# A joint norm factor, context squares moved, and filler matmuls in a two-block transformer kernel

## The reference

```python
def rmsnorm(t, g):
    y = t32 * lax.rsqrt(jnp.mean(t32 * t32, axis=-1, keepdims=True) + EPS)
    return (y * g).astype(t.dtype)
# first block, per layer
px = (rmsnorm(x, norm1_g[l]) * (1.0 + sc1) + sh1) @ w_in[l] + b_in[l]
pc = (rmsnorm(xc, norm1_g[l]) * (1.0 + scc1) + shc1) @ w_in[l] + b_in[l]
# ... mLSTM in both directions, spatial gating, convolution -> y_x, y_c
x = x + g1 * (y_x @ w_out[l])
x = x + g2 * swiglu(rmsnorm(x, norm2_g[l]) * (1.0 + sc2) + sh2, w_gu[l], w_down[l])
# the context gets the same, but not in the block's last layer
return rmsnorm(x, final_g)            # end of the first block
# second block: starts with that x and a new context ctx_2; per layer
hx = _rms(x, norm_mix_w[l]) * (1.0 + scx1) + shx1
hc = _rms(ctx, norm_mix_w[l]) * (1.0 + scc1) + shc1
# ... attention -> x = x + gx1 * ax; x = x + gx2 * _swiglu(...)
```

## Time and profile before

| | us |
|---|---|
| median of 3 runs | 2315.93 (2315.74 to 2325.12) |
| the profiled execution | 2320.48 |
| its span, first to last instruction | 2319.0 |
| mean granted TensorE clock | 0.965 of 2.4 GHz |

### The profile page before, as it was taken

One profiled execution on the slowest core, in us unless ns is written; L12 is line 12 of the kernel. 1 busy time (PEld: TensorE's weight loads), 2 busy tenths in 40 slices (PEclk: granted clock), 3 DMA queues, 4 the chain that ended last, 5 costly groups with the idle time before them and its releaser, 6 DMA issues.

```text
span 2319.0 us, 28203 instructions
## 1 busy us (share of the span) xinstructions
PE 2172.9 (94%) x11748; PEld 1663.5 (72%) x11748; DVE 1100.9 (47%) x1927; ACT 855.5 (37%) x1320; POOL 63.8 (3%) x66
## 2 busy tenths in 40 slices
PE   5999789999999898699979999999999989998999
PEld 2766566777776776699966447677777767747999
DVE  4293854323233666655563433432323355556555
ACT  2434233222222553544444243322222344355443
POOL 1000010000001000100010001000000100000000
PEclk7999789999999999899989999999999999999999
DMA  9553023554446524446535002355344322202564
GB/s 355 172 218 109 1 73 127 172 159 160 163 129 218 161 91 138 136 151 203 161 108 179 35 1 73 127 172 157 125 164 130 107 73 91 73 1 92 177 206 126
DMA packets 263216, 308.08 MB, mean 133 GB/s; under 512 B 5425, under 2 KB 250417, under 8 KB 250801
## 3 DMA queue, kind: packets, MB, share of 16 engines
q1 hardware_dynamic: 258384, 301.62, 39.9%
q10 hardware_dynamic: 4704, 4.65, 0.6%
HBM read 305.21 MB, written 1.05 MB: 132 GB/s over the span
## 4 chain that ended last, share of the span: by engine, by line
PE 86%; DVE 7%; ACT 3%; issue 2%; DMA 1%; POOL 1%; ACTq 0%; POOLq 0%; DVEq 0%
PE bank L458 85%; DVE scratch L1093 1%; POOL yT L435 1%; DVE yT L1093 1%; DVE big L1093 1%; PE bank L467 1%; DMA xT<-p_ctx 1%; DVE weights_low L1101 1%; ACT weights_high L1777 1%; DVE input_low L1093 0%; DVE big L1612 0%; ACT rstd L1803 0%; DVE big L1508 0%; DMA parameter_columns<-p_columns 0%; ACT rstd L1805 0%
## 5 line engine op out<-in xcount | busy, mean ns | idle before, releaser
L458 PE MATMUL bank<-input_high,weights_high 128*128 128x512 f32 (+1 forms) x2336 | 826.3, 354 | 37.1 <-DVE input_low L1093 28.1
L458 PE MATMUL bank<-input_low,weights_high 128*128 128x512 f32 (+1 forms) x2336 | 811.6, 347 | 0.0
L458 PE MATMUL bank<-input_high,weights_low 128*128 128x512 f32 (+1 forms) x2336 | 810.4, 347 | 0.0
L1101 DVE TENSOR_TENSOR weights_low<-weight_slots,weights_high 128x1024 fp32r<-128x1024 f32 (+2 forms) x420 | 461.1, 1137 | 413.0 <-ACT weights_high L1777 412.1
L458 PEld LDWEIGHTS bank<-input_high,weights_high 128*128 128x128 f32 x2336 | 444.8, 190 | 153.1 <-issue 71.6
L458 PEld LDWEIGHTS bank<-input_high,weights_low 128*128 128x128 f32 x2336 | 444.1, 190 | 61.2
L458 PEld LDWEIGHTS bank<-input_low,weights_high 128*128 128x128 f32 x2336 | 444.8, 190 | 58.0 <-issue 1.0
L1777 ACT ACTIVATE weights_high<-weight_slots 128x1024 fp32r<-128x1024 f32 (+2 forms) x420 | 386.3, 967 | 177.6 <-PE bank L458 164.6
L458 PE MATMUL bank<-hidden_high,weights_high 128*128 128x256 f32 (+1 forms) x704 | 239.3, 340 | 0.5 <-DVE weights_low L1101 0.5
L458 PE MATMUL bank<-hidden_low,weights_high 128*128 128x256 f32 (+1 forms) x704 | 237.4, 337 | 0.0
L458 PE MATMUL bank<-hidden_high,weights_low 128*128 128x256 f32 (+1 forms) x704 | 237.2, 337 | 0.0
(11 more groups left out here) (230 smaller groups left out, 1570.3 us busy)
## 6 DMA issues: line engine op xcount, KB each, us to landing
modulation_slots<-w_mod SPq DMA_DIRECT2D x48, 1024.0 KB, 5.0
modulation_slots<-mod_w SPq DMA_DIRECT2D x48, 1024.0 KB, 5.0
weight_slots<-w_gu SPq DMA_DIRECT2D x44, 1024.0 KB, 5.1
weight_slots<-ffn_w_in SPq DMA_DIRECT2D x44, 1024.0 KB, 5.1
weight_slots<-w_in SPq DMA_DIRECT2D x24, 1024.0 KB, 5.5
weight_slots<-w_down SPq DMA_DIRECT2D x16, 768.0 KB, 4.9
weight_slots<-ffn_w_out SPq DMA_DIRECT2D x16, 768.0 KB, 5.0
weight_slots<-od_w_in SPq DMA_DIRECT2D x12, 1024.0 KB, 5.2
```

The lines of the kernel that those rows point to most:

```text
L458: return pe.matmul(o, w, r, start=start, stop=stop, skip_group_check=shared)
L1101: tt(m.w_low[:, g % 2, c], m.ring[:, g % SLOTS, c], m.w_high[:, g % 2, c].bitcast(F32), ALU.subtract).then_inc(m.low_made.sem, 1)
```

## The change

1. `add_squares` and `join_squares` take the semaphores of the squares as a parameter and can carry two kinds of sums (`sq_sum` has two rows).
2. A new function `keep_busy(b, n)` on TensorE issues n float32 matmuls of the 1/1024 matrix with the identity (128 by 128) into a bank that nobody reads: 8 at the start, 12 after the sums in each turn of 512 tokens and after feed forward 1, 9 after mixers 1 and 3.
3. The context's squares are made by ScalarE in hidden tiles 4 to 11 of layer 1 (one per tile); their sum stands before the second part of the down projection, their root at its head.
4. At the end of layer 1 two kinds of squares are made per block, of x and of x times the final gain. VectorE forms EPS*(s1+EPS)+s2 from the two means; one Ln and Exp of that is the joint factor of both norms, and layer 2's x gains are multiplied with the final gain. x itself is scaled by its final norm later, in projection tiles 4 to 11 of layer 2, with a root taken after layer 2's `normed`.
5. At the start the two inputs have a semaphore each; squares, joins and sums are made per half, the sums behind modulation steps 4 and 6. The first half of the second weight item goes from before `normed` into it.

```diff
-        self.sq_sum = self.yT[:, 6, :]
+        self.sq_sum = self.yT[:, 6:8, :]
...
-    join_squares("first", slice(0, TOK))
+    for half, t in enumerate((X, C)):
+        join_squares(("first", half), t, m.first_squared)
...
-        join_squares(("out", L), n)
+        join_squares(("out", L), n, m.squared)
         if L == 1:
-            join_squares("context", C)
+            join_squares("context", C, m.squared)
         if L < 3:
-            join_squares(("ffn", L), n)
-        if L == 1:
-            join_squares("final", X)
+            join_squares(("ffn", L), n, m.squared, 2 if L == 1 else 1)
...
+    def add_squares(place, t, squared=m.squared, banks=(7,)):
+        n = len(banks)
         pe.wait_ge(*m.square_joined.end(place))
+        for q, b in enumerate(banks):
+            mm(bank[b][:, t], m.mean_d[:, :], m.sq_sum[:, q, t], True, False)
+        for q, b in enumerate(banks):
+            i = n * (KD - 1) + q
+            pe.wait_ge(*squared.at(place, i))
+            mm(bank[b][:, t], m.mean_d[:, :], yT[:, 2 + i % 4, t], False, True).then_inc(m.square_added.sem, 1)
+
+    def keep_busy(b, n):
+
+        for _ in range(n):
+            mm(bank[b][:, 0:P], m.mean_d[:, :], ident[:, :], True, True)
...
         add_squares(("out", L), slice(0, n))
+        keep_busy(6, 12 if n == TOK else 9)
...
         hidden(L, range(6, 11))
+        if L == 1:
+            add_squares("context", C, banks=(6,))
         down(L, 1)
-        if L < 3:
+        if L == 1:
+            add_squares(("ffn", L), X, banks=(7, 5))
+            keep_busy(4, 12)
+        elif L < 3:
             add_squares(("ffn", L), slice(0, n))
+            keep_busy(5, 12)
...
     for k in range(KD):
         mod_step(k)
-        if k == 5:
-            add_squares("first", slice(0, TOK))
+        if k in (4, 6):
+            add_squares(("first", k // 2 - 2), (X, C)[k // 2 - 2], m.first_squared)
     pe.wait_ge(*m.columns_in.end(0))
     mod_turn(0)
+    keep_busy(6, 8)
...
             if part and f == KD - 2 and L < 3:
                 gains(L + 1, 0)
+                if L == 1:
+                    dve.wait_ge(*m.gains.at(2, 0))
+                    tt(m.coef[:, 0, 0, :], m.coef[:, 0, 0, :], column(G_TAB, FINAL_G, KD), ALU.mult).then_inc(m.gains.sem, 1)
...
+    def final_scaled(k):
+
+        if k == 0:
+            dve.wait_ge(*m.root.at("final", 1))
+        muladd(xT[:, k, X], xT[:, k, X], column(G_TAB, FINAL_G + k), m.final_r, ALU.mult, ALU.mult).then_inc(m.final_scaled.sem, 1)
...
+            if 4 <= e < 12:
+                final_scaled(e - 4)
...
     def even_mixer(L):
-        normed(0, L, TOK, "final", m.proj[L][1], "context")
+        dve.wait_ge(*m.square_added.at(("ffn", 1), 0))
+        ts(rs[:, X], bank[7][:, X], EPS, EPS, ALU.add, ALU.mult).then_inc(m.final_var.sem, 1)
+        dve.wait_ge(*m.square_added.at(("ffn", 1), 1))
+        dve.wait_ge(*m.final_var.at(0, 0))
+        tt(rs[:, X], rs[:, X], bank[5][:, X], ALU.add).then_inc(m.final_var.sem, 1)
+        normed(0, L, TOK, ("ffn", 1), m.proj[L][1], "context")
...
-    low_weights(1, range(1))
...
-    dve.wait_ge(*m.root.at(("ffn", 1), 1))
-    for k in range(KD):
-        muladd(xT[:, k, X], xT[:, k, X], column(G_TAB, FINAL_G + k), rs[:, X], ALU.mult, ALU.mult).then_inc(m.final_scaled.sem, 1)
...
+    def two_squares(f):
+
+        for q in range(2):
+            i = 2 * f + q
+            if i >= 4:
+                act.wait_ge(*m.square_joined.at(("ffn", 1), 2 * max(0, f - 3) + q))
+            F(yT[:, 2 + i % 4, X], xT[:, f, X], ACT.Square, scale=column(G_TAB, FINAL_G + f) if q else 1.0).then_inc(m.squared.sem, 1)
+
+    def final_roots():
+
+        act.wait_ge(*m.final_var.end(0))
+        F(rs[:, X], rs[:, X], ACT.Ln).then_inc(m.root.sem, 1)
+        act.wait_ge(*m.root.at(("ffn", 1), 0))
+        F(rs[:, X], rs[:, X], ACT.Exp, scale=-0.5).then_inc(m.root.sem, 1)
...
+                if L == 1 and 4 <= f < 4 + KD:
+                    if f == 4:
+                        act.wait_ge(*m.context_in.end(0))
+                    square("context", f - 4, C)
...
+        if part and L == 1:
+            rstd("context", C, 6)
...
+        if L == 1:
+            down(L, 1, two_squares)
+            final_roots()
+            return
...
     def even_mixer(L):
         normed(0, L, TOK, m.proj[L][1])
+        final_root()
...
-        if L == 1:
-            act.wait_ge(*m.context_in.end(0))
-            for k in range(KD):
-                square("context", k, C)
         feed_forward(L)
-    for k in range(KD):
-        act.wait_ge(*m.final_scaled.at(0, k))
-        square("final", k, X)
-    rstd("final", X, 5)
```

More of the change, by code:

```diff
@@ L313, in signals @@
         self.biased, self.gains = S("modulation_thirds_biased", *((l, 3) for l in layers)), S(
[L314 to L326, removed]
+            "norm_gains_made", (0, 4), (1, 4), (2, 5), (3, 4))
+        halves = [("first", half) for half in range(2)]
+        order = [("out", 0), ("ffn", 0), ("out", 1), "context", ("ffn", 1), ("out", 2), ("ffn", 2), ("out", 3)]
+        kinds = {p: 2 if p == ("ffn", 1) else 1 for p in halves + order}
+        self.first_squared = S("first_squares_made", *((p, KD) for p in halves))
+        self.squared = S("squares_made", *((p, KD * kinds[p]) for p in order))
+        self.square_joined, self.square_added = S("squares_joined", *((p, (KD - 2) * n) for p, n in kinds.items())), S(
+            "squares_added", *kinds.items())
+        self.final_var = S("final_variances", (0, 2))
+        self.root = S("rstd_steps", *((p, 2) for p in [
+            "first", ("out", 0), ("ffn", 0), ("out", 1), "context", ("ffn", 1), "final", ("out", 2), ("ffn", 2), ("out", 3)]))
         normed = [x for L in layers for x in (
@@ L1129, in gains, with normed @@
                    ALU.mult).then_inc(m.gains.sem, 1)
-    def normed(which, L, n, place, second, also=None):
+    def normed(which, L, n, place, second, also=None, halves=range(1, 2)):
         part, per = (("mix", "ffn")[which], L), n // SEQ
@@ L1153, in normed @@
             if i == 2 * per - 1:
-                low_weights(second, range(1, 2))
+                low_weights(second, halves)
         for i in range((KD - 1) * per, KD * per):
@@ L1734, in vector_program @@
     dve.memset(m.evac_scale[:, K_T:K_T + 4], HD ** -0.5).then_inc(m.consts.sem, 1)
-    dve.wait_ge(*m.input_in.end(0))
-    for k in range(KD):
-        if k >= 4:
-            dve.wait_ge(*m.square_joined.at("first", max(0, k - 5)))
-        tt(yT[:, 2 + k % 4, :], xT[:, k, :], xT[:, k, :], ALU.mult).then_inc(m.first_squared.sem, 1)
+    for half, t in enumerate((X, C)):
+        dve.wait_ge(m.inputs_in[half], 16)
+        for k in range(KD):
+            if k >= 4:
+                dve.wait_ge(*m.square_joined.at(("first", half), max(0, k - 5)))
+            tt(yT[:, 2 + k % 4, t], xT[:, k, t], xT[:, k, t], ALU.mult).then_inc(m.first_squared.sem, 1)
     low_weights(0)
@@ L1809, in coming_weights, with normed @@
             next_weights(m.proj[L][(e + 1) // 2])
-    def normed(which, L, n, second):
+    def normed(which, L, n, second, halves=range(1, 2)):
         part, per = (("mix", "ffn")[which], L), n // SEQ
@@ L1820, in normed @@
             if i == per - 1:
-                high_weights(second, range(1, 2))
+                high_weights(second, halves)
     def gate_activations(L):
@@ L2184, in scalar_program @@
     ln_exp_tables()
+    act.wait_ge(*m.square_added.end(("first", 0)))
+    act.wait_ge(*m.square_added.end(("first", 1)))
     rstd("first", slice(0, TOK))
```

56 lines of the change are left out of this document (22 added, 34 removed).

## The result

The changed kernel takes 2297.9 us (median of 4 runs, 2296.7 to 2298.3); the kernel before, beside it, 2319.7 (4 runs, 2315.7 to 2325.1). The ratio is 0.9899, 95% interval 0.9881 to 0.9918: 1.0% faster. The forecast was 2291.0 (2282 to 2302).

What follows compares the result with a forecast made beforehand. TensorE, busy 94% of the 2319.0 us span, and its clock were taken to bound the kernel. Terms summing to 24.9 us took 2320.5 to 2295.6, less 4.55 for the median: 2291.0 us, range 2282 to 2302.

Steps and rivals of the forecast that it cites:

- Rival (a): In the turns: the filler doesn't hold the clock, so only 13.5 to 14 us stay, giving 2302 us; chance 0.10.
- The terms for mixer 0, mixer 2 and feed forwards 0 and 2: Restarts behind these turns: held clock gains 2.1, 2.5, 0 (VectorE bounds it) and 1.7 us.
- mixer 3's: Restart behind mixer 3: held clock gains 0.8 us (0 to 1.6), with one 0.6 us stall for a VectorE weight half.
- rival (b): In the gaps: filler at 0.73 us each outlasts the waits and blocks, costing 33 us, giving 2324 us; chance 0.03.
- a sign of being wrong: At the restarts: the prediction is wrong if the first product follows a filler without idle.
- the term of -0.9: Layer 1's second down projection: the moved context sum and ScalarE's root cost 0.9 us (0.4 to 1.8).
- rival (c): Layer 1's hidden tiles: Square forces ScalarE table loads between Silus, hidden but for about 2 us, 2293 us; chance 0.02.
- The turn was sized at 8.8: Turn from layer 1's feed forward to layer 2: the joint factor brings the first product 8.8 us earlier, at 1174.9.
- its clock at 1.9: Behind the joint turn: half of 3.84 us of low clock goes, gaining 1.9 us.
- The step that failed: Layer 1's second down projection: 8 more squares and 6 additions fit 3.5 us periods of which ScalarE uses half, unpriced.
- a sign that came out 0.6 us late: Layer 2's start: first product about 7 us after the last down product instead of 15.7.
- Rival (d): In the mLSTM gaps: shifted work meets half clock elsewhere, either sign, 10 us at the bad end, 2301 us; chance 0.07.

Runs made afterwards that it cites:

- the two-norm version: Changed kernel with the joint factor undone: final norm applied and its own squares taken after layer 1's feed forward, 12 fillers behind each sum; 2306.4 us.
- the two experiments on it: Changed kernel with ScalarE's squares put behind the next high weights, 2298.7 us; changed kernel with GpSimd's second-kind additions cut to one column, 2295.7 us.
- the version with small additions: Changed kernel with GpSimd's additions of the second kind of square in layer 1's feed forward cut to one column, sums left incomplete; 2295.7 us.

## Why the prediction came out as it did

- **Clock and filler.** Right: 0.237 us each for 0.25 estimated, 1.00 behind all seven turns with VectorE's wait left over, and 8.5 us lost in the restarts, 10.3 in all stretches, where the filler is taken away. Rival (a), that it doesn't hold the clock, is refuted by the pair of clock rows. The terms for mixer 0, mixer 2 and feed forwards 0 and 2 are within 0.35 us; mixer 3's, 0.2 for 0.8, allowed VectorE one stall of 0.6 us, where the trace has 0.73 and slower steps behind it (0.92 and 0.81 us for the 0.7 assumed). The filler's half-clock price stood in rival (b), "the filler blocks"; not foreseen is where it is met: 0.47 us each at the start and 0.39 in the two-norm version. There (b) is real, on a scale of 1 us and not of 33. That the first product at the start then follows a filler without idle is a sign of being wrong that did occur, in that one place.
- **Context squares.** Right to 0.1 us in the turn and to 0.15 in the term of -0.9. Of its 1.05 us, 0.67 is the sum; the other 0.38 isn't the squares, as the restart behind mixer 1 takes 15.54 us against 15.16 before the first of them is made, and the products behind it keep their pace (980 further records in 114.33 and 114.34 us). Another 0.3 in the down projection is left when the joint factor is undone, and fits the context's root. No table load stands among the hidden tiles, so rival (c) is gone.
- **Joint factor.** The turn was sized at 8.8 and is 8.8; its clock at 1.9 and is 1.6. The step that failed is the one that priced the second squares at nothing, "in 3.5 us periods of which ScalarE uses half". A busy share doesn't say that. The loop was a ring of dependent work (add, square, high half, low half) and the trace of before had only 0.32 us of slack in it, the wait that TensorE ended before each add. One more square of 0.40 us used that up, and 0.3 us of slower low weights overran it. The projection took 2.2 us more: the two experiments on it gave back 1.5 and 1.6, undoing the joint factor 1.9, and the remaining 0.3 fits the context's root. It also explains a sign that came out 0.6 us late: the first product was to stand about 7 us behind the last down product, and stands 7.6 behind it.
- **What shifts.** Rival (d), half clock met elsewhere, came in small: -1.9 us at layer 2's attention in the profiled run, of which a repetition had 0.4, and +1.5 in layer 1's mLSTM. That they nearly cancel is luck.
- **The start.** Its 3.0 us against 1.3 can't be split: the same code varied by 3.0 us up to that landmark. What the earlier sum of squares gives alone wasn't tried.
- **The median.** Of the 6.9 us between 2291.0 and 2297.9, the sum's excess is 2.7. The rest is the subtraction of 4.55 us for a profiled run above the median. Three runs of before, two at 2316 and one at 2325, didn't bear it: with more of them its median is 2319.7 to 2321.8, where the profiled one lies. Since the base was some 4 us low, the whole time alone wouldn't have told the forecast from rival (a), which had 2302: the repetitions are at 2300.7 and 2301.6. The clock rows told them apart.

Open are the whole time of the undone context squares (9 to 12 us by medians, 7.5 in the profile), what decides in an execution whether the clock falls at the attention's start, and why a repetition took 1.4 us more between the same products at granted clock 1.00.

## What to carry to other kernels

Work that goes "beside" a loop must be held against the slack of the loop's longest ring of dependent instructions, read as the idle time that the pacing engine ends in it, and not against busy shares. Filler that keeps TensorE's clock is worth half of the cold stretch behind a wait if TensorE bounds that stretch, and nothing if another engine does; it must start right behind the last matmul and stand where a wait is, and it must end before the wait does where TensorE sets the pace behind it. Shorten a turn first and fill it then: behind the two shortened turns here filler gave 3.3 us, behind the same turns unshortened 1.1.

## Not expected of the hardware

- The clock fell after waits in which TensorE did run matmuls: idle pieces of 1.13, 0.34 and 1.76 us between matmuls, and then 3.4 us at half clock in one execution of the changed kernel and none in another.
- Early in layer 0's mLSTM the same code had 10.2 us at half clock in the changed kernel's profile (227.1 to 237.3) and granted clock 1.00 from 230 to 235 in the version with small additions:

```profile
230.00:235.00 5.00, 2.75 (x16) 1.00 0.00 0
```

- Two of the five last executions of the changed kernel took 5499 and 8632 us. In the latter's trace a group of product records of 512 and 256 columns takes 1056 ns on the mean, three times the 352 of the changed kernel's usual profile, while VectorE's add keeps its 0.48 us, and the granted clock reads 1.00 (0.41 in the other one, which has no trace):

```profile
L455 PE MATMUL bank<-input_high,weights_high 128*128 128x512 f32 (+1 forms) x2336 | 2467.3, 1056 | 3.9 <-DVE input_low L1429 3.9
```

The other engines kept their pace (VectorE busy 1112.5 us against 1100.8, ScalarE 861.3 against 854.8); which limit this is the trace doesn't say.
